# Attention kernel: which PSUM bank stands aside, and one feature turn a step sooner

## The chip, the cores and the metric

The kernel runs on one core of a Trainium2 chip. The metric is the device time of one execution in microseconds (us): the median of several runs. TensorE does the matmuls and writes only to PSUM, which has eight banks of 128 partitions x 512 float32 here (`ps[:, b, :]`). VectorE (DVE), ScalarE (ACT) and GpSimd (POOL) do the elementwise work, SyncE (SP) issues the weight transfers.

## The reference, cut to what matters

Two blocks one after the other on 256 tokens of width 1024, in float32. The first block has a pooling mixer and a dilated window attention (three groups of 16 heads). The second has two layers with modulation rows from a condition, each a mixer and an MLP; the first layer works on 256 tokens and 256 context tokens.

```python
# second block, layer 0: two attentions whose outputs stand side by side
o_a = gqa_attend(qa_x, ka_all, va_all)              # "A": 8 heads, 2 key heads
a = p[:, :, 0] - lam * p[:, :, 1]                   # "B": 4 heads, pairs of softmaxes
o_b = rms_norm(einsum('bhqs,bshe->bqhe', a, v), subln_g) * (1 - lam0)
out_x = concatenate([o_a, o_b], -1) @ w_out
# layer 1: "C" (window and sink, 8 heads), "D" (neighbourhood with bias, 8 heads)
# every layer: x = x + g1 * rms_norm(mixer); x = x + g2 * rms_norm(mlp)
```

## The kernel before, in words

Every float32 product is made of three matmuls of rounded high and low halves (`mm3`, lines 573 to 575; by halves at 620 and 622). Weights come as one stream of 1 MB chunks (`raw`, three slots, issued on SP at L539). ScalarE makes the high half (L1151), VectorE the low half (L1167); modulation rows use the raw chunk in TensorE directly (`mod`, L703). A chunk's slot is loaded again once it was used.

TensorE's program is one sequence of jobs written out by hand. `job(...)` (L561) gives a job its PSUM bank: the next of a list (`state["banks"]`, counter `turn[0]`), and makes TensorE wait until the job that had the bank before was read. A bank's reader is ScalarE or VectorE, each with a fixed order of its own.

An attention (`attend`, L842) runs over items, each a head and a tile of 128 queries. Step i issues the scores of the items ahead (L755, for the first attention L747), then side jobs placed by step, then the turned probabilities (`turns`, L789) of item i - lag and the product with the values (`values`, L817) of item i - lag - 1. The lag is 3 in A and 2 elsewhere. A and the first attention issue the scores of two items in every other step; in B one item has two score tiles. In the kernel before the banks in an attention are:

- first attention: the list is 0 to 5; side jobs take 6 and 7 in turn (`side=1`) until step 24, when both go back into the list's head;
- A and B of layer 0: the list is the other seven in order of last use; bank 7 stands aside (`side=2`) for projection blocks spread over the steps: in A two query tiles of the next part (`query_block`), in B from step 8 the first output tile (`product_block`). After A bank 7 becomes the list's first, after B its last;
- C and D of layer 1: as the first attention, until step 16.

The jobs ahead of A, in order (from L1044): key tile 2, four turned features `n1` (L658), key tile 3, query tile 0, query tile 1, in the midst of which the turned queries 2 and 3 and keys 2 and 3 (`turn_heads`, L1022) stand. Then A's step 0 issues the scores of items 0 and 1 and key tile 0, step 1 key tile 1. A query tile is read by ScalarE (L1595, squares) and then by VectorE (`head_sums`: L2334 and two of L2339); a turned tile is read by ScalarE (L1583).

In B, `side_steps_pairs` (L452) places turns of the feature-wise mixer output `fo` for the output projection: turn 0 in step 5, turn 1 in step 6, turns 2 and 3 in steps 16 and 17. A turn is four transposes (L658), a copy of the high half on ScalarE (L1215) and the low half on VectorE (L1777), which is the bank's last read. In a step VectorE does the maxima of two score tiles (L1998), combines the pair of the item before (L2043, L2044, L2046; this gives the probabilities), reads the output of item i - 4 (L2064) and makes the low half of a turn of that step. ScalarE copies the turned probabilities (L1340), makes the exponents (L1321) and then the turn's high half.

Of the kernel before, what the change touches and what calls it, by code (L numbers as in the profile page):

```python
# [278 lines left out]
def build(nc, T, out, counts):  # L279
    did, after = counts.did, counts.after  # L280
    with ExitStack() as ctx:
# [74 lines left out]
        mix = tile(ctx, "mix", [P, 4, D])  # L356
# [95 lines left out]
        def side_steps_pairs():  # L452


            return ([(1, ("v2", 0, 1, 0)), (3, ("v2", 0, 1, 1))] + [(at, ("fo", j)) for j, at in enumerate((5, 6, 16, 17))]
                    + [(8 + k, ("product", k)) for k in range(4)]
                    + [(18 + n, ("weights", PLACE[UNIT["out2", 0, 1].w0] + n)) for n in range(2)])

# [95 lines left out]
        def _(pe):  # L554
            mm = nc.tensor.matmul
            last = {}
            turn = [0, 0, 0]
            state = {"banks": list(range(8))}

            def job(*label, side=0):  # L560

                banks = (state["banks"], (6, 7), (7,))[side]
                b = banks[turn[side] % len(banks)]
                turn[side] += 1
                if b in last:
                    pe.wait_ge(*after("read", *last[b]))
                last[b] = label
                counts.banks[label] = b
                return ps[:, b, :]
# [75 lines left out]
                    ins = mm(o[:, 0:rhs.shape[-1]], lhs, rhs, start=True, stop=True)  # L645
                ins.then_inc(*did("tensor", ("read", "spin", label)))

            def turn_feature(name, src, tiles, ready, j):

                o = job(name, j)  # L650
                if j == 0:
                    for r in ready:
                        pe.wait_ge(*after(*r))
                for q in range(2):
                    for i, t in enumerate(tiles):
                        k = 2 * j + q
                        c = (2 * q + i) * P
                        ins = nc.tensor.transpose(o[:, c:c + P], src(t)[:, k * P:k * P + P], ident[:, :])  # L658
                ins.then_inc(*did("tensor", (name, j)))
# [6 lines left out]
            def turn_mixed(l, g, j):  # L666

                tiles = (2 * g, 2 * g + 1)
                ready = []
                if j == 0:  # L670
                    ready = [("mixed out" if l else "first half out", l, t) for t in tiles]
                elif l == 0 and j == 2:
                    ready = [("mixed out", l, t) for t in tiles]
                for r in ready:
                    pe.wait_ge(*after(*r))
                turn_feature(("fo", l, g), lambda t: mix[:, t, :], tiles, [], j)

            pending = []

# [140 lines left out]
            def query_block(t, k):  # L820

                u, name = UNIT["q2", 0, 1], ("q2", 0, 1, t)
                o = job(*name, side=2) if k == 0 else ps[:, counts.banks[name], :]
                if t == 2:
                    wait_weights(u, k)
                ins = mm3(o, fhi[:, k, t * P:t * P + P], flo[:, k, t * P:t * P + P],
# [5 lines left out]
            def product_block(k):  # L832

                u, name = UNIT["out2", 0, 0], ("out2", 0, 0, 2)
                o = job(*name, side=2) if k == 0 else ps[:, counts.banks[name], :]
                wait_weights(u, k)
                wait_feature(("fo", 0, 1), k)
                mm3(o, fhi[:, k, 2 * P:3 * P], flo[:, k, 2 * P:3 * P],
                    whalf(whi, u, k, 0, NW), whalf(wlo, u, k, 0, NW), k == 0, False)

            def attend(items, mods, steps=()):

                lag = turned_behind(items)
                for i in range(len(items) + lag + 1):
# [1 line left out]
                    if i < len(items) and i % ahead == 0:  # L846
                        scores(items[i:i + ahead])
                    alone = items[0][0] in ("first", "C") and i >= len(items) - (8 if items[0][0] == "first" else 16)
                    if alone and len(state["banks"]) == 6:

                        state["banks"] = [6, 7] + [state["banks"][(turn[0] + n) % 6] for n in range(6)]
                        turn[0] = 0
                    for at, step in steps:
                        if step[0] in ("chunk", "bias", "weights", "roots", "ahead", "queries"):
                            continue
# [91 lines left out]
            for n in range(2):  # L947
                by_token(UNIT["gb", n], ("gb", n), range(XT))

            state["banks"] = list(range(6))  # L950
            attend(items_first(), [], side_steps())
            turn_mod()
            turn_features("fo1", lambda t: gb[:, t, :], (0, 1), [("gated", items_first()[-1])])
# [59 lines left out]
            for l in range(2):  # L1013
# [12 lines left out]
                for part in range(2 - l):  # L1026
# [32 lines left out]
                    beside = l == 1  # L1059
                    if beside:  # L1060
                        gate_rows(1)
                    if beside:
                        state["banks"] = list(range(6))
                    else:
                        oldest = [state["banks"][(turn[0] + n) % 8] for n in range(8)]
                        state["banks"], turn[0] = [b for b in oldest if b != 7], 0
                    attend(items_second(l, part), mods_second(l, part),
                           side_steps_last() if beside else side_steps_pairs() if part else side_steps_halves())
                    if l == 0:
                        oldest = [state["banks"][(turn[0] + n) % 7] for n in range(7)]  # L1070
                        state["banks"], turn[0] = oldest + [7] if part else [7] + oldest, 0
                    else:
                        state["banks"] = list(range(8))
                if l == 0:
                    for n in range(2):
                        by_token(UNIT["out2", 0, n], ("out2", 0, n), (2, 3), feat=None if n else ("fo", 0, 1), last=False,
# [42 lines left out]
                for t in range(XT):  # L1119
                    for n in range(2):  # L1120
                        held[t, n] = job("acc", t, n)
                state["banks"] = [b for b in range(8) if b not in [counts.banks[("acc", t, n)] for t in range(2) for n in range(2)]]
                mlp_out(1, 0, range(2), ns=(0,), last=False)
                turn_hidden(1, 1)
                mlp_out(1, 0, range(2), ns=(1,), first=False)
# [1614 lines left out]
```

## Time and profile before

| | |
|---|---|
| median of three runs | 1545.56 us (1544.12 to 1545.67) |
| the profiled execution | 1544.99 us, span 1543.0 us |
| TensorE busy | 1508.7 us, 98% |
| TensorE weight loads busy | 1251.7 us, 81% |
| VectorE, ScalarE, GpSimd busy | 59%, 43%, 11% |
| granted clock of TensorE | 0.999 of full over the span |
| weight stream | 210 transfers of 1 MB, mean 151 GB/s |

The span is the time between the first and the last instruction; the device time has some 2 us more. A busy TensorE is not one at its peak, as its records are modelled and overlap. A row of the order of time gives start, duration, engine, line, tiles (out<-in), shape and count, and in brackets the idle time before it with the engine and line that ended it.

### The profile page before, as it was taken

Reading aid. Unit: us, or ns where it says so; the run is one execution under the profiler, and the core shown is the slowest. Engines: PE = TensorE matmul, PEld = TensorE weight load, DVE = VectorE, ACT = ScalarE, POOL = GpSimd, SP = SyncE. Lnnn points to the kernel's source line nnn. Section 1 sums busy time; section 2 is a strip of 40 time slices with the busy share of each in tenths; the row PEclk is TensorE's granted clock in tenths of the full one; section 3 lists DMA queues with packets and bytes.
Section 4 is the critical chain, followed back from the end, with each engine's and each line's share of the span. In section 5 each row is a group of like instructions: output and inputs, shape, how many; then the busy total and the mean of one; then the engine's idle time right before and its main releaser. Section 6 shows DMA issues by size and latency. Waiting matters only on the chain.

```text
span 1543.0 us, 22914 instructions
## 1 busy us (share of the span) xinstructions
PE 1508.7 (98%) x8906; PEld 1251.7 (81%) x8906; DVE 904.6 (59%) x1550; ACT 656.3 (43%) x1025; POOL 166.9 (11%) x179
## 2 busy tenths in 40 slices
PE   9999999999999998999999999999999999999998
PEld 7998698889897775786899777777787887778886
DVE  5785674756565883546675343333448646667655
ACT  5464334444444544536554222231224546654342
POOL 2200220000000120001223100111012020001010
PEclk9999999999999999999999999999999999999999
DMA  6456564453536225220232353443512421155451
GB/s 246 187 203 235 223 224 174 172 191 141 188 124 259 110 95 209 110 79 32 83 137 96 128 213 144 183 181 147 201 72 92 148 76 55 69 177 219 182 199 55
DMA packets 43765, 233.73 MB, mean 151 GB/s; under 512 B 13265, under 2 KB 14225, under 8 KB 16785
## 3 DMA queue, kind: packets, MB, share of 16 engines
q1 hardware_dynamic: 31232, 222.38, 38.4%
q10 hardware_dynamic: 12432, 9.94, 2.2%
q8 instruction: 72, 1.18, 0.3%
q14 instruction: 29, 0.23, 0.0%
HBM read 231.22 MB, written 1.08 MB: 151 GB/s over the span
## 4 chain that ended last, share of the span: by engine, by line
PE 86%; DVE 8%; ACT 2%; issue 1%; POOL 1%; DMA 1%; SPq 0%; DVEq 0%; ACTq 0%
PE ps L573 19%; PE ps L575 19%; PE ps L574 19%; PE ps L620 9%; PE ps L817 5%; PE ps L622 4%; PE ps L789 3%; DVE wlo L1167 3%; PE ps L755 2%; PE ps L703 2%; PE ps L747 2%; POOL f L2580 1%; DMA raw<-in_wstream 1%; PE ps L687 1%; ACT whi L1151 1%
## 5 line engine op out<-in xcount | busy, mean ns | idle before, releaser
L1167 DVE TENSOR_TENSOR wlo<-raw,whi 128x2048 fp32r<-128x2048 f32 x150 | 347.0, 2333 | 186.8 <-ACT whi L1151 186.5
L1151 ACT ACTIVATE whi<-raw 128x2048 fp32r<-128x2048 f32 x162 | 305.4, 1907 | 236.8 <-PE ps L575 162.4
L573 PE MATMUL ps<-whi,f 128*128 128x512 f32 (+1 forms) x624 | 221.9, 356 | 6.4 <-DVE dev L1815 2.6
L575 PE MATMUL ps<-whi,f 128*128 128x512 f32 (+1 forms) x624 | 216.1, 346 | 0.0
L574 PE MATMUL ps<-wlo,f 128*128 128x512 f32 (+1 forms) x624 | 215.8, 346 | 0.0
L573 PE MATMUL ps<-f,whi 128*128 128x256 f32 (+1 forms) x640 | 206.8, 323 | 1.8 <-DVE wlo L1167 1.6
L620 PE MATMUL ps<-f,whi 128*128 128x512 f32 x576 | 203.1, 400 | 2.8 <-DVE kq L1983 1.6
L575 PE MATMUL ps<-f,wlo 128*128 128x256 f32 (+1 forms) x640 | 205.0, 320 | 0.0
L574 PE MATMUL ps<-f,whi 128*128 128x256 f32 (+1 forms) x640 | 204.9, 320 | 0.0
L573 PE MATMUL ps<-whi,hhi 128*128 128x512 f32 x384 | 152.6, 397 | 0.0
L575 PE MATMUL ps<-whi,hlo 128*128 128x512 f32 x384 | 151.9, 395 | 0.0
L574 PE MATMUL ps<-wlo,hhi 128*128 128x512 f32 x384 | 151.8, 395 | 0.0
L573 PEld LDWEIGHTS ps<-whi,f 128*128 128x128 f32 x624 | 118.1, 189 | 33.3 <-issue 9.6
L622 PE MATMUL ps<-f,wlo 128*128 128x256 f32 x504 | 141.4, 280 | 0.0
L573 PEld LDWEIGHTS ps<-f,whi 128*128 128x128 f32 x640 | 121.8, 190 | 20.3 <-issue 6.5
L575 PEld LDWEIGHTS ps<-whi,f 128*128 128x128 f32 x624 | 118.1, 189 | 14.9
L575 PEld LDWEIGHTS ps<-f,wlo 128*128 128x128 f32 x640 | 121.9, 190 | 8.9
L574 PEld LDWEIGHTS ps<-f,whi 128*128 128x128 f32 x640 | 121.9, 190 | 8.6
L574 PEld LDWEIGHTS ps<-wlo,f 128*128 128x128 f32 x624 | 118.3, 190 | 12.6
L620 PEld LDWEIGHTS ps<-f,whi 128*128 128x128 f32 x576 | 104.8, 188 | 27.7 <-issue 3.8
L2591 POOL TENSOR_TENSOR hlo<-htmp,hhi 128x256 fp32r<-128x256 f32 (+1 forms) x64 | 60.5, 945 | 423.9 <-ACT hhi L1518 423.9
L622 PEld LDWEIGHTS ps<-f,wlo 128*128 128x128 f32 x504 | 95.2, 189 | 2.5
(282 smaller groups left out, 2147.5 us busy)
## 6 DMA issues: line engine op xcount, KB each, us to landing
raw<-in_wstream SPq DMA_DIRECT2D x210, 1024.0 KB, 4.9
gates<-gated ACTq DMA_DIRECT2D x6, 512.0 KB, 4.2
hx<-in_x SPq DMA_DIRECT2D x1, 1024.0 KB, 5.4
lnrow<-in_ln_g ACTq DMA_DIRECT2D x2, 512.0 KB, 4.1
lnrow<-in_ln_b ACTq DMA_DIRECT2D x2, 512.0 KB, 5.7
hc<-in_ctx ACTq DMA_DIRECT2D x1, 1024.0 KB, 5.5
mix<-in_rpb_rows ACTq DMA_DIRECT2D x4, 256.0 KB, 4.4
hc<-in_rpb_rows ACTq DMA_DIRECT2D x4, 256.0 KB, 3.8
```

Of the source, the lines that this page charges most:

```text
L573: mm(o, lh, rh, start=start, stop=False)
L574: mm(o, lh, rl, start=False, stop=False)
L575: return mm(o, ll, rh, start=False, stop=stop)
L620: ins = mm(both, wh, parts_f[:, :, k, c0:c0 + S], start=k == 0, stop=k == KD - 1)
L622: mm(o[:, 0:S], wl, fhi[:, k, c0:c0 + S], start=False, stop=False)
L703: ins = mm(o[at:at + 32, :], condz[:, 2 * k:2 * k + 32], raw[:, c % RAW_SLOTS, base:base + NW], start=k < 4, stop=k >= 4, tile_position=(0 ...
L747: ins = mm(o, kq1[po:po + DH, l % 2, 1, j * 2 + tq, t * P:t * P + P], kq1[po:po + DH, l % 2, 0, j * 2 + tq, 0:n], start=True, stop=True)
L789: ins = nc.tensor.transpose(o[:, (j - b) * P:(j - b + 1) * P], e[:, j * P:j * P + P], ident[:, :])
L817: ins = mm(o[:, 0:dv], p[:, i % 2, j * P:j * P + P], v, start=j == 0, stop=j == kt - 1)
L1151: nc.scalar.activation(whi[:, w % SPLIT_SLOTS, :], raw[:, c % RAW_SLOTS, :], ACT.Copy, scale=QSCALE if SPLIT[w][0].name[0] == "q" else 1.0 ...
L1167: ins = nc.vector.tensor_tensor(low, raw[:, c % RAW_SLOTS, :], high, ALU.subtract)
L2591: p.tensor_tensor(hlo[:, j % 2, e, cols], htmp[:, e % 2, cols], hhi[:, j % 2, e, cols].bitcast(F32), ALU.subtract).then_inc(*did("pool", * ...
```

## The change

It rewrites how banks are put aside. `set_aside(n)` takes the n banks used longest ago out of the list, for side jobs; `bring_back` puts them at the list's head, or at its end. Lists are turned so that their first is the one used longest ago, also after the last accumulators have taken their banks. A side job with nothing aside takes from the list with the list's counter. In A and B the bank aside is thus no longer always bank 7. The turns 0 and 1 of `fo` in B take the bank aside, and turn 0 goes from step 5 to step 4, on TensorE, ScalarE and VectorE.

```diff
-            return ([(1, ("v2", 0, 1, 0)), (3, ("v2", 0, 1, 1))] + [(at, ("fo", j)) for j, at in enumerate((5, 6, 16, 17))]
+            return ([(1, ("v2", 0, 1, 0)), (3, ("v2", 0, 1, 1))] + [(at, ("fo", j)) for j, at in enumerate((4, 6, 16, 17))]
...
-            turn = [0, 0, 0]
-            state = {"banks": list(range(8))}
+            turn = [0, 0]
+            state = {"banks": list(range(8)), "aside": []}
+
+            def oldest_first():
+                return [state["banks"][(turn[0] + n) % len(state["banks"])] for n in range(len(state["banks"]))]
+
+            def set_aside(n):
+                banks = oldest_first()
+                state["aside"], state["banks"], turn[:] = banks[:n], banks[n:], [0, 0]
+
+            def bring_back(last=False):
+                banks = oldest_first()
+                state["banks"] = banks + state["aside"] if last else state["aside"] + banks
+                state["aside"], turn[:] = [], [0, 0]
 
             def job(*label, side=0):
-                banks = (state["banks"], (6, 7), (7,))[side]
+                side = 1 if side and state["aside"] else 0
+                banks = state["aside"] if side else state["banks"]
                 b = banks[turn[side] % len(banks)]
...
-                turn_feature(("fo", l, g), lambda t: mix[:, t, :], tiles, [], j)
+                turn_feature(("fo", l, g), lambda t: mix[:, t, :], tiles, [], j, side=1 if (l, g) == (0, 1) and j < 2 else 0)
...
-                o = job(*name, side=2) if k == 0 else ps[:, counts.banks[name], :]
+                o = job(*name, side=1) if k == 0 else ps[:, counts.banks[name], :]
...
-                    if alone and len(state["banks"]) == 6:
-                        state["banks"] = [6, 7] + [state["banks"][(turn[0] + n) % 6] for n in range(6)]
-                        turn[0] = 0
+                    if alone and state["aside"]:
+                        bring_back()
...
-            state["banks"] = list(range(6))
+            set_aside(2)
             attend(items_first(), [], side_steps())
...
-                    if beside:
-                        state["banks"] = list(range(6))
-                    else:
-                        oldest = [state["banks"][(turn[0] + n) % 8] for n in range(8)]
-                        state["banks"], turn[0] = [b for b in oldest if b != 7], 0
+                    set_aside(2 if beside else 1)
                     attend(items_second(l, part), mods_second(l, part),
                            side_steps_last() if beside else side_steps_pairs() if part else side_steps_halves())
-                    if l == 0:
-                        oldest = [state["banks"][(turn[0] + n) % 7] for n in range(7)]
-                        state["banks"], turn[0] = oldest + [7] if part else [7] + oldest, 0
-                    else:
-                        state["banks"] = list(range(8))
+                    if not beside:
+                        bring_back(last=part == 1)
...
-                state["banks"] = [b for b in range(8) if b not in [counts.banks[("acc", t, n)] for t in range(2) for n in range(2)]]
+                standing = [counts.banks[("acc", t, n)] for t in range(2) for n in range(2)]
+                state["banks"], turn[0] = [b for b in oldest_first() if b not in standing], 0
```

## Rows read from the trace of the kernel before

**Rows 1.** The page: busy time by engine, TensorE's granted clock in 40 slices
```profile
PE 1508.7 (98%) x8906; PEld 1251.7 (81%) x8906; DVE 904.6 (59%) x1550; ACT 656.3 (43%) x1025; POOL 166.9 (11%) x179
...
PEclk9999999999999999999999999999999999999999
```

**Rows 2.** TensorE's waits over the whole span: total, times, longest, in us
```profile
PE ps L620 <- DVE kq L1983: 1.6, 1, 1.6
```

**Rows 3.** First attention in order of time, TensorE and then VectorE
```profile
471.50 1.92 PE L703 MATMUL ps<-raw,condz 128*32 128x512 f32 x16
473.71 0.52 PE L789 MATMUL ps<-ident,e 128*128 128x128 f32 x3 [0.30 <-DVE modsum L1906]
...
473.39 0.18 DVE L1906 TENSOR_REDUCE modsum<-ps 128x8 f32<-128x32 f32 x1
```

**Rows 4.** A attention's start, TensorE in order of time
```profile
561.73 0.70 PE L755 MATMUL ps<-kT,qT 64*128 64x256 f32 x4
562.73 0.38 PE L573 MATMUL ps<-whi,f 128*128 128x256 f32 x1 [0.30 <-DVE mix L2339]
...
565.71 0.28 PE L573 MATMUL ps<-whi,f 128*128 128x256 f32 x1
```

**Rows 5.** The same stretch on VectorE
```profile
561.93 0.74 DVE L2339 TENSOR_TENSOR mix<-ps,ropeg 128x256 f32<-128x256 f32 x2
...
564.64 0.74 DVE L2339 TENSOR_TENSOR mix<-ps,ropeg 128x256 f32<-128x256 f32 x2
...
567.60 0.29 DVE L2329 TENSOR_REDUCE hss<-e 128x2 f32<-128x128 f32 x1 [0.63 <-ACT e L1595]
...
569.41 0.76 DVE L1998 TENSOR_REDUCE nmax<-ps 128x1 f32<-128x256 f32 x2 [0.61 <-PE ps L755]
...
571.19 2.28 DVE L1167 TENSOR_TENSOR wlo<-raw,whi 128x2048 fp32r<-128x2048 f32 x1
```

**Rows 6.** The chain near 574 us (start, us, what), and TensorE at 582
```profile
574.50 7.63 DMA raw<-in_wstream
...
582.17 1.06 PE L703 MATMUL ps<-raw,condz 128*32 128x512 f32 x8 [1.24 <-DMA raw<-in_wstream]
```

**Rows 7.** B attention, TensorE in order of time
```profile
707.62 0.70 PE L755 MATMUL ps<-kT,qT 64*128 64x256 f32 x4
...
710.38 0.63 PE L658 MATMUL ps<-ident,mix 128*128 128x128 f32 x4 [0.40 <-DVE mix L2064]
...
712.15 0.70 PE L755 MATMUL ps<-kT,qT 64*128 64x256 f32 x4 [0.48 <-ACT e L1321]
...
713.82 0.71 PE L817 MATMUL ps<-vv,p 128*128 128x128 f32 x4 [0.17 <-DVE f L1777]
715.69 0.70 PE L755 MATMUL ps<-kT,qT 64*128 64x256 f32 x4 [1.15 <-DVE mix L2064]
...
719.00 0.38 PE L789 MATMUL ps<-ident,e 128*128 128x128 f32 x2
```

**Rows 8.** B attention, VectorE in order of time
```profile
709.89 0.35 DVE L2064 TENSOR_SCALAR mix<-ps,rinv 128x128 f32<-128x128 f32 x1
710.15 0.75 DVE L1998 TENSOR_REDUCE nmax<-ps 128x1 f32<-128x256 f32 x2
...
711.66 0.35 DVE L2064 TENSOR_SCALAR mix<-ps,rinv 128x128 f32<-128x128 f32 x1
713.08 0.69 DVE L1777 TENSOR_TENSOR f<-ps,f 128x512 fp32r<-128x512 f32 x1 [1.07 <-ACT f L1215]
...
716.01 0.69 DVE L1777 TENSOR_TENSOR f<-ps,f 128x512 fp32r<-128x512 f32 x1 [0.47 <-ACT f L1215]
...
718.12 0.35 DVE L2064 TENSOR_SCALAR mix<-ps,rinv 128x128 f32<-128x128 f32 x1
...
729.67 1.29 DVE L1998 TENSOR_REDUCE nmax<-ps 128x1 f32<-128x512 f32 x2 [0.63 <-PE ps L755]
```

**Rows 9.** B attention, ScalarE in order of time: the turn's copy
```profile
712.44 0.60 ACT L1215 ACTIVATE f<-ps 128x512 fp32r<-128x512 f32 x1
```

More of the change, by code:

```diff
@@ L646, in spin, with turn_feature @@
                 ins.then_inc(*did("tensor", ("read", "spin", label)))
-            def turn_feature(name, src, tiles, ready, j):
-                o = job(name, j)
+            def turn_feature(name, src, tiles, ready, j, side=0):
+                o = job(name, j, side=side)
                 if j == 0:
@@ L834, in product_block @@
                 u, name = UNIT["out2", 0, 0], ("out2", 0, 0, 2)
-                o = job(*name, side=2) if k == 0 else ps[:, counts.banks[name], :]
+                o = job(*name, side=1) if k == 0 else ps[:, counts.banks[name], :]
                 wait_weights(u, k)
```

## The prediction

> **What bounds the kernel now.** The page's first part comes first [rows 1]: TensorE is busy for 1508.7 of 1543.0 us, and its granted clock is at the full level (2.4 GHz) in every slice. All its idle time is 34.3 us, so no edit of banks can be worth more; what matters is which single waits of TensorE it removes or makes. The view of TensorE's waits says who ended them: its largest by a key tile of the first attention is 1.6 us [rows 2]; in the A attention it is exponents of ScalarE and one weight transfer, in the pairwise (B) attention VectorE's reads of outputs. Then I read the order of time at three places, TensorE's side and the releaser's [rows 3 to 9].
>
> A job starts when the job that had its bank before was read. So two times count for each: when TensorE could come to it, and when the bank's last read ended. The change computes the same; it pairs jobs with other banks and brings one turn forward. I went through the jobs in the code's order, gave each its bank by the old and by the new rule, and looked where the new last read ends after TensorE comes, and where an old wait of that kind goes. Three places came out.
>
> **First attention.** Two banks stand aside before and after, and each side job follows the side job two before it, as now: the 1.6 us wait stays. What changes is behind the banks' return at step 24. Before, a turn of the modulation row still counted over banks 6 and 7 by itself although both were back in the list, and the second job after it was given the bank it had just filled: the transposes at 473.71 idle 0.30 us for the read that starts at 473.39 and takes 0.18 [rows 3]. After, the turn is counted with the others and the transposes get an output's bank that was read long before. They follow the 16 modulation matmuls (471.50, 1.92 us) directly. Bounds 0 and 0.3; I take 0.3, as TensorE has no other wait for the next 20 us.
>
> **A attention, the new wait.** The last eight takers of banks before it are, oldest first: the fourth turned feature of n1, key tile 3, query tile 0, query tile 1, two query turns, two key turns. Before, the list without bank 7 gives the first score the feature's bank, the second key tile 3's, and key tile 0 of step 0 query tile 0's. The trace bears it out: that tile's first matmul (562.73) idles 0.30 us for L2339 [rows 4], which is query tile 0's last read, two instructions from 561.93 in 0.74 us, over at 562.67 [rows 5]. After, the oldest bank is the one set aside and all move up one: the scores get key tile 3's and query tile 0's banks, key tile 0 gets query tile 1's. Its last read is the same pair of instructions at 564.64, over at 565.38 [rows 5], and VectorE, which has no idle time ahead of it, can't do it sooner. So the scores wait from 561.73 to 562.7, and the key tile starts at 565.42 (0.04 behind the read, as 562.73 is to 562.69) instead of 562.73: 2.7 us. Both waits lie on one path, so it is 2.7 and not 2.7 + 1.0.
>
> Queued behind it on TensorE are key tile 1 (565.71, its new bank a query turn's, long read) and all of step 2. Who waits for these: VectorE idles 0.63 us at 567.60 for ScalarE's square of key tile 0 and 0.61 us at 569.41 for step 2's scores, and from there runs through to the low half of weights at 571.19 [rows 5], which releases a weight slot. The transfers behind it are issued by 574.50 and land 7.63 us later, and TensorE idles 1.24 us for them at 582.17 [rows 6]. So the transfers are issued 2.7 us later too, and the idle time stays 1.24: that is why I count nothing of the 2.7 as absorbed. What idle time follows in A is for exponents of scores that TensorE itself issued, and shifts with it. Bounds: 2.7, and 2.7 - 1.24 = 1.5 if the transfer came at its old time. I take 2.7.
>
> **B attention, the moved turn.** Now turn 0 of `fo` stands in step 5 and takes the next of seven banks, whose output is read by 710.24 (709.89 + 0.35): it starts at 710.38 after 0.40 us idle. Its bank then holds up a product by 0.17 us, and the scores of steps 6 and 7 idle 0.48 and 1.15 us for the banks of outputs 1 and 2 [rows 7]. In all 2.20 us of TensorE's idle time lie here. After, in the old frame of time (all is 2.4 us later by then):
> - The turn stands behind step 4's scores (707.62 and some 0.64) and its bank was read long ago: 708.26 to 708.70 (its issue takes 0.46 here: 710.38 to the next 710.84). Step 5's scores start at 709.48.
> - ScalarE's exponents of step 4 come 0.25 later, as the turned probabilities ahead of them do. Its copy follows and ends at 711.0 [rows 9]. VectorE reads output 0 by 710.24 as now, waits for the copy, and makes the low half from 711.04 to 711.73. Step 5's maxima then start at 711.64 instead of 710.15, and output 1 is read by 713.50 instead of 712.01 (711.66 + 0.35) [rows 8].
> - Step 6's scores no longer need that bank: 711.14 instead of 712.15. Turn 1 follows when turn 0's low half is done, 711.9. But step 6's turned probabilities need output 1's bank: 713.6, 0.3 later than now. The wait has moved by one job.
> - Step 7's scores start at 714.40 instead of 715.69, its turns when output 2 is read (715.28), at 715.42.
> - Step 8's turns need output 3. VectorE waits 0.80 and 0.65 us for the two copies where it waited 1.07 and 0.47, so it is only 0.1 earlier here: output 3 is read by 718.40 (718.12 + 0.35 - 0.08), start 718.50 instead of 719.00 [rows 7, 8].
>
> So of the 2.20 us only 0.5 come through: VectorE's order, not the banks, is what ends last. From 719.00 on TensorE has no idle time up to step 12's scores and keeps the 0.5; VectorE idles 0.63 for those scores at 729.67 [rows 8], which then come 0.5 sooner, and carries it on. Bounds: 0.1 (VectorE's share alone) and 2.2 (every wait gone); I take 0.5. The turn's own time, ScalarE's 0.60 and VectorE's 0.69 are the same work moved by a step; none of it issues anything on SP's or POOL's queue.
>
> **The rest.** C/D takes the two oldest banks instead of 6 and 7, and the list behind the last accumulators is in another order. Every job there that comes within 0.5 us of its bank's last read has the same predecessor before and after: 0.
>
> **Sum.** -0.3 + 2.7 - 0.5 = +1.9 us. Against the profiled execution's 1544.99 (its span 1543.0 and 1.99 around it) this is 1546.9; that execution lies 0.57 under the median of three, 1545.56, so for a median the forecast is 1547.4. That is +0.12%, less than the 0.2% (3.1 us) that a measurement of this kernel can tell from no change.
>
> **The rivals.**
> - *The wait in A is absorbed.* For it: an idle time of 1.24 us for a transfer stands close behind. Against: the transfer's issue hangs on VectorE, which waits for the late tiles. It gives 1547.4 - 1.24 = 1546.2. Chance 0.12.
> - *No new wait in A, or all of B's go.* If the list stood otherwise at A's start: 1547.4 - 2.7 = 1544.7; with all of B's 2.2 besides: 1543.0. Against: the 0.30 us row names the query tile. Chance 0.08.
> - *Slower, by the order on VectorE in B.* Turn 0's low half now stands before step 5's maxima. If ScalarE's copy comes late, every later output read is late by it. It decides from the point where step 8's turns come after 719.00: the two waits for copies then add up to 2.0 us or more instead of 1.45. With one whole copy and low half (0.60 + 0.69) not hidden, B costs 0.8 instead of giving 0.5: 1548.7, and 1549.0 without the first attention's 0.3. Chance 0.13.
> - *The clock falls.* TensorE would idle 1.0 and 2.0 us around four short matmuls. After the trace's 1.6 us idle at a key tile the clock stayed at its full level [rows 1, 2]. Were it at 1.2 GHz for as much work as lies between 565.71 and A's first turns, some 5.4 us, that would cost up to 5.4: 1552.8. Chance 0.02. The Trainium skill ("TensorE: Matmul & The Clock Gate", section "A second HAM failure mode: psum-queue depth-cycling") says that cycling through PSUM banks can leave TensorE idle so often that the clock swings between its levels. By that rule this rival, and against it the trace: B now has four such idle times within 6 us at the full clock.
> - *It doesn't do what it says*: the banks come out in another order than worked out, and the waits are as before, 1545.6. Chance 0.03.
>
> **How the numbers follow.** The forecast has 0.62, with a range of its own of 1546.3 to 1548.5. Faster by over 0.2% (under 1542.5) is a part of the second rival: 0.03. Slower by over 0.2% (over 1548.65): the third and fourth and 0.04 of the forecast's own spread, 0.19. Within it: 0.78. The range reaches down into the second rival and up through the third: 1543.9 to 1549.6.
>
> **What would show it.** In the profile after: around 561.4 to 565.1 the scores idle about 1 us and key tile 0 about 2, both for L2339; no wait of L789 for L1906; up to 690 everything later than before by 2.4. In B: turn 0 directly behind step 4's scores; in place of the 1.15 us of the scores (L755) for L2064 a wait of about 1.3 us of the probabilities' turns (L789) for L2064 in step 6; VectorE's two waits for L1215 together some 1.45 us. I would be wrong if the key tile waits under 1 us, or if the distance to before shrinks or grows between 570 and 600 us.

## The result, and the profile after

| | before | after |
|---|---|---|
| median of 10 runs each | 1545.80 us (1543.98 to 1547.30) | 1550.02 us (1548.61 to 1550.54) |
| ratio, 95% interval | | 1.0027 (1.0020 to 1.0035) |
| profiled execution, its span | 1544.99, 1543.0 us | 1549.87, 1548.0 us |
| granted clock over the span | 0.999 | 0.996 |

The changed kernel is slower, by 4.2 us in the medians and 4.9 us in the profiled executions. The forecast was 1547.4 us with a range up to 1549.6: the sign was right, the size was not, and the time lies 0.4 us outside the range.

The page of after, its line of busy times, has the same work on each engine as [rows 1] and 3.5 us more of TensorE's busy time. The same number of matmuls is busy for longer, so some of them ran slower:

```profile
PE 1512.2 (98%) x8906; PEld 1254.8 (81%) x8906; DVE 904.7 (58%) x1550; ACT 656.4 (42%) x1025; POOL 166.9 (11%) x179
```

Both kernels have 8906 records of matmuls in the same roles, so I subtracted the start of each one before from its start after. Below, "late" is that difference. These are the places at which it could move.

**First attention.** The matmuls of the modulation row stand at 471.33 now, and the transposes behind them no longer wait as in [rows 3]: late goes from -0.17 to -0.53. At 486.67 it is back at 0.00, where both kernels start the second half of the next modulation row. Now it idles there, for a transfer (TensorE in order of time):

```profile
486.67 1.07 PE L719 MATMUL ps<-raw,condz 128*32 128x512 f32 x8 [0.32 <-DMA raw<-in_wstream]
```

**A's start.** TensorE in order of time, the rows that answer [rows 4], and then the releaser on VectorE, which answers [rows 5]:

```profile
562.87 0.70 PE L771 MATMUL ps<-kT,qT 64*128 64x256 f32 x4 [1.03 <-DVE mix L2347]
565.49 0.58 PE L589 MATMUL ps<-whi,f 128*128 128x256 f32 x1 [1.91 <-DVE mix L2347]
...
566.29 0.41 PE L589 MATMUL ps<-whi,f 128*128 128x256 f32 x1
566.51 0.41 PE L590 MATMUL ps<-wlo,f 128*128 128x256 f32 x1
...
569.28 0.28 PE L591 MATMUL ps<-whi,f 128*128 128x256 f32 x1
569.40 0.28 PE L589 MATMUL ps<-whi,f 128*128 128x256 f32 x1
```
```profile
564.69 0.74 DVE L2347 TENSOR_TENSOR mix<-ps,ropeg 128x256 f32<-128x256 f32 x2
```

The scores (L771) wait 1.03 us and key tile 0 (L589) waits 1.91, both for a query tile's last read (L2347 is before's L2339, and starts at 564.69 as it did at 564.64). The key tile starts 2.75 us late. Then look at the distance of its matmuls, two rows with the same 256 columns: 0.22 us at 566.3, 0.12 us at 569.3. The view by stretches gives the granted clock (the fourth figure, behind the count: 1.00 is the full 2.4 GHz, 0.50 is 1.2 GHz):

```profile
core 0: us, PE busy (x), PEclk, DMA share, GB/s
561.00:565.00 4.00, 1.54 (x8) 1.00 0.68 252
565.00:569.00 4.00, 3.51 (x18) 0.57 0.03 10
569.00:573.00 4.00, 4.00 (x34) 1.00 0.00 0
```

From 565.1 to 568.5 the clock was at 1.2 GHz, behind two idle times with four short matmuls between them. At 568.43 late is 4.04: the fall, the stretch at the lower clock, cost 1.3 us more.

**The transfer at 582.17** [rows 6] is met at 586.10 with 1.11 us idle instead of 1.24, and late goes from 4.06 to 3.92.

**B.** TensorE in order of time, the rows that answer [rows 7]:

```profile
712.17 0.66 PE L674 MATMUL ps<-ident,mix 128*128 128x128 f32 x4
...
714.30 0.41 PE L805 MATMUL ps<-ident,e 128*128 128x128 f32 x2 [0.17 <-DVE mix L2072]
...
717.51 0.41 PE L805 MATMUL ps<-ident,e 128*128 128x128 f32 x2 [1.13 <-DVE mix L2072]
...
719.28 0.41 PE L805 MATMUL ps<-ident,e 128*128 128x128 f32 x2 [0.28 <-DVE mix L2072]
...
722.38 0.41 PE L805 MATMUL ps<-ident,e 128*128 128x128 f32 x2 [0.29 <-DVE mix L2072]
```

Turn 0 stands directly behind step 4's scores. The four waits of before, 2.20 us, are gone, and four others have come, 1.87 us, all of the transposes of p for VectorE's output reads (L2072, before's L2064). Late falls from 3.9 at 707.62 to 3.38 at 719.00. VectorE's waits for the two copies are 0.75 and 0.64 us, together 1.39 (1.45 forecast):

```profile
714.90 0.69 DVE L1785 TENSOR_TENSOR f<-ps,f 128x512 fp32r<-128x512 f32 x1 [0.75 <-ACT f L1223]
...
719.77 0.69 DVE L1785 TENSOR_TENSOR f<-ps,f 128x512 fp32r<-128x512 f32 x1 [0.64 <-ACT f L1223]
```

**Around 1360 us** both kernels idle some 2.4 us (2.34 before, 2.37 after) ahead of a first unit of the last MLP. Behind it the clock fell in after's profile (0.60 of full between 1364 and 1368 us) and not in before's; late goes from 3.5 to 5.0 and stays there.

The sum of the profiled executions: 0 + 2.75 + 1.3 - 0.1 (the transfer) - 0.5 + 1.6 = 5.05 us, beside 5.0 us between the spans. The last 1.6 looked as if it had nothing to do with the change; the experiments had to say that, and whether the 1.3 had.

### The profile page after: what moved, and what is told of

Read it like the earlier page. It is cut to its first block, busy times and chain, and to the rows that moved or that the text cites. A ratio compares the mean times of both kernels' runs of the same rounds, so it can differ in the third digit from the quotient of the medians.

```text
span 1548.0 us, 22914 instructions
## 1 busy us (share of the span) xinstructions
PE 1512.2 (98%) x8906; PEld 1254.8 (81%) x8906; DVE 904.7 (58%) x1550; ACT 656.4 (42%) x1025; POOL 166.9 (11%) x179
## 4 chain that ended last, share of the span: by engine, by line
PE 86%; DVE 8%; ACT 2%; DMA 2%; issue 1%; POOL 1%; SPq 0%; DVEq 0%; ACTq 0%
PE ps L589 19%; PE ps L591 19%; PE ps L590 19%; PE ps L636 9%; PE ps L833 5%; PE ps L638 4%; PE ps L805 3%; DVE wlo L1175 3%; PE ps L719 3%; PE ps L771 2%; DMA raw<-in_wstream 2%; PE ps L763 1%; POOL f L2588 1%; PE ps L703 1%; ACT whi L1159 1%
## 5 line engine op out<-in xcount | busy, mean ns | idle before, releaser
L589 PE MATMUL ps<-whi,f 128*128 128x512 f32 (+1 forms) x624 | 223.1, 357 | 8.1 <-DVE dev L1823 2.6
L589 PE MATMUL ps<-f,whi 128*128 128x256 f32 (+1 forms) x640 | 206.8, 323 | 1.8 <-DVE wlo L1175 1.6
L589 PE MATMUL ps<-whi,hhi 128*128 128x512 f32 x384 | 152.6, 397 | 0.0
L589 PEld LDWEIGHTS ps<-whi,f 128*128 128x128 f32 x624 | 119.1, 191 | 35.1 <-issue 9.0
L589 PEld LDWEIGHTS ps<-f,whi 128*128 128x128 f32 x640 | 121.8, 190 | 20.3 <-issue 6.5
```

Of the source, the lines that this page charges most:

```text
L589: mm(o, lh, rh, start=start, stop=False)
```

## The experiments

Each ratio is to runs of the kernel before on the same chip. Those runs have medians of 1545.57 us (experiments 1, 2, 4 and 5), 1545.71 (3, 6, 7 and 9), 1545.22 (8, 10 and 11) and 1545.84 (12), the last two on one chip. So where experiments from different sets are compared, some 0.6 us of a difference may be the set's. A ratio is not that of the two medians, and differs from it by up to 0.9 us.

**1. A's bank alone (a_fifth).** The changed kernel, in which A sets aside the bank that it had before.

```diff
-            def set_aside(n):
+            def set_aside(n, at=0):
                 banks = oldest_first()
+                banks = [banks[at]] + banks[:at] + banks[at + 1:] if at else banks
...
-                    set_aside(2 if beside else 1)
+                    set_aside(2 if beside else 1, at=0 if beside or part else 4)
```

> The changed kernel, but ahead of the A attention the fifth oldest bank is set aside (a query turn's, as before the change) instead of the oldest. Theory (the new wait for the query tiles' last reads and the lower clock behind it are the whole loss): the waits for L2339 shrink from 2.9 to 0.3 us, the clock does not fall near 565 us, and the time is about 2.7 + 1.3 = 4.0 us under the changed kernel's 1550.0, so 1545.4 to 1546.2, ratio to before 0.9998 to 1.0003. Rival (the loss has another place, such as the order of banks elsewhere): at least 1547.5, ratio over 1.001.

Measured: 1545.31 us (1542.95 to 1546.35), ratio 0.9994 (0.9985 to 1.0003). The key tile waits as in [rows 4], and no clock falls there (TensorE in order of time):

```profile
562.70 0.39 PE L590 MATMUL ps<-whi,f 128*128 128x256 f32 x1 [0.30 <-DVE mix L2348]
```

So one bank at one place holds the whole loss: in the medians 4.2 us above before with it, 0.3 below without. The rest of the change gives too little to be told from nothing.

**2. The other way round (before_a_oldest).** The kernel before, with only A's bank taken as the oldest.

```diff
-                banks = (state["banks"], (6, 7), (7,))[side]
+                banks = (state["banks"], (6, 7), state["one"])[side]
...
-                        state["banks"], turn[0] = [b for b in oldest if b != 7], 0
+                        state["one"] = (7,) if part else (oldest[0],)
+                        state["banks"], turn[0] = [b for b in oldest if b != state["one"][0]], 0
```

> The kernel before with one part of the change alone: in the A attention the bank set aside is the one used longest ago instead of bank 7. Theory: this makes the whole loss and nothing of the gains, so slightly slower than the changed kernel: 1545.8 + 2.7 + 1.3 = 1549.8, or 1550.2 if the changed kernel's B gain of 0.4 us is real; a clock fall behind the wait near 565 us. Rival (the loss comes from several parts): under 1548.5.

Measured: 1556.44 us (1554.31 to 1557.51), ratio 1.0071 (1.0057 to 1.0085). That is over 6 us more than either expectation, and more than the whole change costs. A's two waits and the fall of the clock behind them are there. But there is a new one, ahead of the first scores of layer 1's attention, which in before and after wait 0.62 us for a turned key tile. TensorE and then VectorE in order of time:

```profile
1214.30 1.22 PE L755 MATMUL ps<-kT_b,qT_b 64*128 64x512 f32 x2 [4.87 <-DVE grow L2159]
```
```profile
1208.87 2.29 DVE L1168 TENSOR_TENSOR wlo<-raw,whi 128x2048 fp32r<-128x2048 f32 x1
1211.56 2.29 DVE L1168 TENSOR_TENSOR wlo<-raw,whi 128x2048 fp32r<-128x2048 f32 x1 [0.40 <-ACT whi L1152]
1213.77 0.27 DVE L2159 COPY grow<-ps 32x128 f32<-32x128 f32 x1
```

By the releaser that the trace names, the scores got the bank of the gate row (`grow`) that TensorE had just filled, and VectorE reads that one behind two low halves of weights. The kernel before rotates over banks 0 to 5 there, a fixed list; which of them was used last depends on everything before, and A's other order shifted it. The clock fell behind this wait too, for another 1.5 us.

**3. The fixed banks at layer 1 alone (c_fixed).** To see whether that is it: the changed kernel with banks 6 and 7 aside at layer 1, as before had it.

```diff
-                    set_aside(2 if beside else 1)
+                    if beside:
+                        state["banks"], state["aside"] = list(range(6)), [6, 7]
+                    else:
+                        set_aside(1)
```

> The changed kernel, in which the attention of layer 1 (C, D) sets aside banks 6 and 7 as in the kernel before, and rotates over banks 0 to 5, instead of the two used longest ago. Theory (once A's rotation differs, the fixed banks at layer 1 no longer suit, and C's first scores wait for VectorE's gate rows, as in before_a_oldest): a wait of 4 to 5 us ahead of C's first scores at about 1210 us, 1553 to 1555 us. Rival (the loss in before_a_oldest came from the particular order that it left behind, which this kernel doesn't have): no new wait there, 1549.6 to 1550.4 us.

Measured: 1553.68 us (1553.31 to 1556.04), ratio 1.0057 (1.0041 to 1.0072). The same VectorE copy is waited for, one job later (TensorE in order of time):

```profile
1212.74 0.58 PE L589 MATMUL ps<-f,whi 128*128 128x256 f32 x1 [2.92 <-DVE grow L2171]
```

So the time is as expected and the wait, expected at 4 to 5 us, is 2.9; with the lower clock that its profile has behind it, the cost is 3.7 us in the medians (8.0 us above before, where after is 4.2). The part of the change that I had put at nothing is worth that much here: with A's order as the change makes it, a fixed list at layer 1 costs that again.

**4. The moved turn alone (turns_old).** The changed kernel with turns 0 and 1 back in steps 5 and 6 and in the rotation.

```diff
-[(at, ("fo", j)) for j, at in enumerate((4, 6, 16, 17))]
+[(at, ("fo", j)) for j, at in enumerate((5, 6, 16, 17))]
...
-                turn_feature(..., tiles, [], j, side=1 if (l, g) == (0, 1) and j < 2 else 0)
+                turn_feature(..., tiles, [], j)
```

> The changed kernel with turns 0 and 1 of fo back in steps 5 and 6 and in banks of the list. Theory (VectorE's order lets 0.5 us of the 2.2 through): 0.5 us slower than the changed kernel, 1550.5; the B attention's four idle times of the kernel before stand again. Rival (all idle time removed there would come through): 2.2 slower, 1552.2. Rival (the moved turn gives nothing): 1550.0.

Measured: 1549.61 us (1547.48 to 1550.82), ratio 1.0023 (1.0014 to 1.0032). The expected 1550.5 did not come: in the medians it isn't above after, so they don't show B's gain. The traces do: B's waits are before's again (0.41, 0.48, 0.17, 1.15 us), and against after's start of B it loses 0.5 us by the end of step 8. A half microsecond lies below what these runs resolve. (The granted clocks of its eleven runs average 0.9968, those of after's ten 0.9961. By my estimate after loses 1.1 us of full clock more by that, 0.0007 of 1548, which is enough to hide it.)

**5. The waits in A filled (wait_filled).** The changed kernel with 8 more matmuls of 256 columns ahead of A's first scores and 15 ahead of key tile 0, into the bank that stands aside. Nothing reads them.

```diff
+                    if i == 0 and items[0][0] == "A":
+                        fill(8, True, False)
...
+                            if at == i == 0:
+                                fill(15, False, True)
```

> The changed kernel with 8 matmuls of 256 columns ahead of A's first scores and 15 ahead of key tile 0, into the bank that stands aside, whose results nobody reads: some 2.7 us of TensorE work in the 2.9 us in which it would wait anyway. The waits and their ends stay where they are. Theory (the clock falls because TensorE idles): no clock fall near 565 us, key tile 0's matmuls 0.12 us apart again, and 1.3 us faster than the changed kernel, 1548.7. Rival (the fall has nothing to do with the idle time, or does not matter): the same as the changed kernel, 1550.0, or slower if the dummy work is in the way.

Measured: 1548.45 us (1547.00 to 1549.29), ratio 1.0015 (1.0006 to 1.0024), 1.6 us less than after (1.3 when the medians are taken against before's, 1.9 by the two ratios). The key tile starts no earlier, but now runs at the full clock. TensorE in order of time, and the stretch that had 0.57:

```profile
563.83 2.06 PE L862 MATMUL ps<-whi,f 128*128 128x256 f32 x15
565.82 0.39 PE L589 MATMUL ps<-whi,f 128*128 128x256 f32 x1
```
```profile
565.00:569.00 4.00, 4.00 (x34) 1.00 0.08 33
```

One profile could be luck, but the granted clocks of its eleven runs average 0.9980, like those of 89 runs of before (0.9979) and unlike those of after's ten (0.9961).

Experiment 3 gives the same split without added work, as c_fixed is the changed kernel up to layer 1. It has both waits and its clock stayed up (TensorE in order of time, and its stretch):

```profile
565.54 0.39 PE L589 MATMUL ps<-whi,f 128*128 128x256 f32 x1 [1.91 <-DVE mix L2352]
```
```profile
565.00:569.00 4.00, 3.46 (x29) 1.00 0.02 8
```

Between 555 and 579 us c_fixed loses 2.7 us to before, wait_filled 2.7 and after 4.0. So about 2.7 us are the wait for the bank, and 1.3 to 1.6 are the clock behind it.

**6. The kernel before, profiled again (before_again).**

> The kernel before, profiled again. If the half-clock stretch at about 180 or 1360 us belongs to idle times that both kernels have, it may show here too, though the first profile had none; near 565 us there is none, since TensorE isn't idle for longer than 0.3 us there. 1544 to 1547 us.

Measured: 1546.86 us, span 1544.9. Of the first two profiles only after's had a stretch at 1.2 GHz near 180 and near 1360 us. In this one the kernel before has both. The idle times ahead of them stand in before's first profile too, where the clock stayed up (TensorE in order of time):

```profile
178.48 1.94 PE L658 MATMUL ps<-ident,hx 128*128 128x128 f32 x16 [2.08 <-DVE hx L1954]
...
1359.34 0.47 PE L573 MATMUL ps<-whi,f 128*128 128x512 f32 x1 [2.34 <-DVE dev L1815]
```

The second profile's view by stretches (busy time of TensorE, its weight loads, VectorE, ScalarE and GpSimd, then granted clock, DMA share, GB/s):

```profile
178.00:183.00 5.00, 4.32 (x24) 3.63 (x28) 3.59 (x8) 1.26 (x2) 1.85 (x2) 0.66 0.93 392
1360.00:1364.00 4.00, 4.00 (x12) 3.14 (x11) 3.86 (x5) 1.09 (x2) 0.00 (x0) 0.57 0.90 314
```

The fall near 180 us costs 1.6 us and is given back by 187, where TensorE would else wait 0.91 and 0.28 us for GpSimd. The one at 1360 costs 1.6 against before's first profile and stays. So the last 1.6 us of the sum above belong to neither kernel: an execution of either has them or not.

**7. The long idle times filled (kept_busy).** a_fifth with matmuls of 128 columns in the two idle times that both kernels have.

```diff
                 o = job(name, j, side=side)
+                if name == "f1" and j == 0:
+                    for _ in range(14):
+                        mm(o[:, 0:P], ident[:, :], ident[:, :], start=True, stop=True)
```

and 16 of the same ahead of the unit at 1355 us.

> The changed kernel with A's bank as before (a_fifth), and matmuls of 128 columns, never read, put into the two longest idle times of TensorE outside A: 14 ahead of the first turn at about 178 us (idle 2.08 us), 16 ahead of the first unit at about 1355 us (idle 2.37 us). They go into the bank that the next group overwrites. Theory (the clock at 1.2 GHz follows an idle time, and at these two places falls in some executions only): the granted clock stays at 2.4 GHz at both, for up to 1.3 us where it fell before; the median falls 0.3 to 1.3 us below a_fifth's 1545.3, so 1544.0 to 1545.0 us. Rival (the fall is not tied to the idle time, or the matmuls themselves delay the path): 1545.3 to 1546.0 us, and a half-clock stretch at the same places.

Measured: 1545.19 us (1544.89 to 1545.75), ratio 1.0000 (0.9991 to 1.0009). The clock stayed at its full level in the profile, and the spread of eleven runs fell from a_fifth's 3.4 us to 0.9. The clock is as the theory had it; the median, expected at 1544.0 to 1545.0, didn't move. The filling was too long (3.39 us of matmuls in an idle time of 2.08 us), which experiment 8 tests.

**8. The right amount (busy_half).** The same with 8 and 9.

> kept_busy with 8 and 9 matmuls instead of 14 and 16: there each was recorded as two of 0.12 us, so that the 28 took 3.39 us of an idle time of 2.08 us and the 32 took 3.73 us of 2.37 us, and TensorE itself came 1.1 to 1.2 us late. Now they take 1.9 and 2.1 us. Theory: the granted clock stays at 2.4 GHz at both places, without the delay: about 1 us below kept_busy's 1545.2, so 1543.6 to 1544.4 us, with a spread of the runs under 1.5 us (that of a_fifth is 3.4 us). Rival (the delay cost nothing, or a clock that falls there costs nothing): 1545.0 to 1545.5 us.

Measured: 1544.36 us (1543.98 to 1544.91), ratio 0.9992 (0.9983 to 1.0001). TensorE in order of time, and its granted clock (1.00) by stretch:

```profile
1356.47 2.17 PE L612 MATMUL ps<-ident 128*128 128x128 f32 x18
1358.85 0.50 PE L590 MATMUL ps<-whi,f 128*128 128x512 f32 x1 [0.21 <-DVE wlo L1182]
```
```profile
1360.00:1364.00 4.00, 4.00 (x23) 1.00 0.83 297
```

It is 0.8 us below kept_busy, near the 1 us expected (0.3 when the medians are taken against before's on each chip, 1.2 by the two ratios); the spread stays at 0.9 us. But the fastest runs of a_fifth (1542.95) and of before (1543.24) are faster than its fastest: the filling takes away the slow executions, and also something from the fastest. The second row also corrects a reading of the profiles without filling, here a_fifth's (TensorE, then VectorE):

```profile
1358.03 0.47 PE L590 MATMUL ps<-whi,f 128*128 128x512 f32 x1 [2.37 <-DVE dev L1824]
```
```profile
1355.59 2.29 DVE L1176 TENSOR_TENSOR wlo<-raw,whi 128x2048 fp32r<-128x2048 f32 x1
```

They put this idle time down to `dev`, a short VectorE operation. In busy_half the releaser is the low half of the next weights, and in a_fifth that one too ends just ahead, at 1357.88.

**9. VectorE's order in B (low_later).** The claim of the prediction's working was that VectorE's order, not the banks, ends last in B. a_fifth, with the low halves of turns 0 and 1 made one step later:

```diff
-                        if at == i and step[0] == "fo":
+                        if step[0] == "fo" and at + (1 if step[1] < 2 else 0) == i:
                             low_feature(("fo", 0, 1), 1, step[1])
```

> The changed kernel with A's bank as the kernel before has it (a_fifth), and VectorE makes the low halves of feature turns 0 and 1 one step later than ScalarE makes the high ones. The operations are the same and only VectorE's order in B differs. Theory (what ends last in B is VectorE's order, not the bank): VectorE no longer stands 0.74 us and 0.64 us waiting for ScalarE's high half, and TensorE's wait for VectorE before the transposes of p behind turn 1 (1.13 us) falls under 0.5 us; 0.6 to 1.4 us less than a_fifth's 1545.3, so 1543.9 to 1544.7 us. Rival (the low half of 0.69 us is only paid a step later, where VectorE again ends last): 1545.0 to 1545.6 us, the idle time moved to a later step.

Measured: 1544.62 us (1542.77 to 1546.00), ratio 0.9993 (0.9984 to 1.0002). The wait of 1.13 us and those behind it are gone, and two of another kind have come (TensorE in order of time):

```profile
711.33 0.66 PE L675 MATMUL ps<-ident,mix 128*128 128x128 f32 x4 [0.90 <-DVE f L1786]
...
715.84 0.50 PE L590 MATMUL ps<-whi,f 128*128 128x512 f32 x1 [0.69 <-DVE f L1786]
```

B gets 0.35 us shorter than a_fifth's by this (-0.64 at its start, -0.98 behind step 8); the other 0.6 between the two profiles is the transfer at 581 us, which TensorE met without waiting. The claim holds for the waits of the transposes; the gain in the trace is smaller than expected, since turn 1 now waits for turn 0's low half in the one bank aside. The median lies within the expected 1543.9 to 1544.7, but in the profile the transfer gave more of it than B.

**10. Turn 1 back in the rotation (low_list).** low_later with only turn 0 aside (`j < 1`), to take those two waits away.

> low_later, with feature turn 1 in a bank of the rotation and only turn 0 in the bank aside. In low_later TensorE waits 0.90 us ahead of turn 1 and 0.69 us ahead of the first product block, both for the low half that frees the bank aside. Theory: both waits go (the bank aside is free, the next bank of the rotation was read some 2 us earlier) and VectorE is next: 0.7 to 1.5 us below low_later's 1544.6, so 1543.1 to 1543.9 us. Rival (VectorE is the bound of these steps, so the time comes back ahead of the transposes of p): 1544.3 to 1544.8 us.

Measured: 1546.92 us (1546.22 to 1548.75), ratio 1.0013 (1.0004 to 1.0022), 2.3 us above low_later (2.8 when the medians are taken against before's). TensorE in order of time:

```profile
711.47 0.66 PE L675 MATMUL ps<-ident,mix 128*128 128x128 f32 x4 [0.30 <-DVE mix L2073]
...
713.93 0.70 PE L772 MATMUL ps<-kT,qT 64*128 64x256 f32 x4 [1.14 <-DVE mix L2073]
...
717.39 1.53 PE L772 MATMUL ps<-kT,qT 64*128 64x512 f32 x4 [1.94 <-ACT subtmp L1399]
```

Both expectations fall. The two waits are gone, but a turn in the rotation of seven moves every later job to a bank that was used one job later, and scores wait 1.14 and 1.94 us. The releaser named for the second reads no bank; turn 1's low half ends 0.25 us before it (716.46, 0.68), and which bank it was I didn't settle. Behind it the clock fell again (718.0), and 1546.9 follows.

**11. Both (low_list_busy)** is low_list with busy_half's matmuls.

> low_list with the matmuls of busy_half. Theory: the two gains lie at different places and add: 1541.8 to 1543.2 us, below both kernels. Rival (one of them is taken back by a transfer behind it, as the first attention's 0.3 us was): 1543.5 to 1544.5 us.

Measured: 1548.17 us (1547.05 to 1549.84), ratio 1.0017 (1.0008 to 1.0026), outside both expectations. Its base had already lost; at 718.4 us the clock stayed low for twice as long as in low_list. Filling the idle times elsewhere doesn't help against a fall that has its own idle time.

**12. The best of the parts (low_later_busy)** is low_later with 8 and 8 matmuls.

> low_later (A's bank as before, the low halves of turns 0 and 1 a step later) with 8 and 8 of the matmuls of busy_half. Theory (the two lie at different places and add): busy_half's 1544.4 less low_later's 0.7 us, so 1543.3 to 1544.0 us, with a spread under 1.5 us and a clock of 1.0, faster than the kernel before by 0.1%. Rival (the time saved in B shifts the later work against the transfers and the clock, as in low_list_busy, which came out 1.3 us above low_list): 1544.4 to 1546 us.

Measured: 1544.22 us (1543.90 to 1544.94), ratio 0.9989 (0.9980 to 0.9998). It falls between the two expectations. It is the fastest median, and the only one below before's whose interval excludes no change; the gain is 0.1%. The granted clock is 0.999 or 1.0 in all eleven runs, which fits a gain from the clock but does not size it. VectorE's order adds 0.1 us to busy_half's 1544.36, less than can be told from nothing.

## Why the prediction was wrong

- *First attention, -0.3.* The wait went as said (0.36 us), but it did not reach the end. The step that failed is "TensorE has no other wait for the next 20 us": it looked only at waits that before had, and with TensorE earlier the weight transfer became the later one, 13 us on. The profiles of after, a_fifth, wait_filled and low_list_busy have 0.32, 0.39, 0.42 and 0.58 us idle there. In all eleven profiles of kernels with this part of the change the 0.36 are there at 474 us, and 0.2 to 0.8 us are lost again by 555. So the net lies between 0.2 us gained and 0.5 lost, never at the 0.3 forecast.
- *A's new wait, +2.7.* Right: 1.03 and 1.91 us idle, 2.75 us late, by the releaser named. Experiment 1 took the wait away and the loss went with it.
- *The transfer absorbs nothing.* Right for after (1.11 us against 1.24). But this idle time isn't fixed by the kernel's order: before has 1.24 and 1.33 in its two profiles, a_fifth and low_later, which are alike up to there, have 0.46 and under 0.1, and after, c_fixed and turns_old, again alike, have 1.11, 1.22 and 0.86.
- *B, -0.5.* Right in size and in its parts: the 1.13 us wait of the transposes, the copies' 1.39, 0.5 us in all. It can be read in the traces only; the medians of experiment 4 don't resolve it.
- *The rest, 0.* In after no new wait came at layer 1, as said. What the sentence missed is that this part of the change does something: without it, experiment 3, the change costs 3.7 us more.
- *The clock.* This is the main step that failed: the sum has no term for it, and the runs show 1.3 to 1.6 us. It stood among the rivals with a chance of 0.02 and a price of up to 5.4 us, and the argument against it was a single idle time of 1.6 us and B's four shorter ones, behind which one profile had the clock up. That profile also has idle times of 2.08 and 2.34 us with the clock up; the second profile of before has the clock down behind both. So one profile without a fall says little. The case was another, too: two idle times close together with almost no work between. In three of the four profiles with that pair the clock fell (after, turns_old and before_a_oldest; not c_fixed), for 1.3 to 1.5 us; experiment 5 filled the idle time without shortening the wait and had 1.3 to 1.9 us back. The chance was far too low, the price four times too high. The Trainium skill ("TensorE: Matmul & The Clock Gate", section "A second HAM failure mode: psum-queue depth-cycling") describes idle times from cycling through PSUM banks that make the clock swing between its levels. The trace of after agrees in part: behind 1.03 and 1.91 us of waiting for banks the clock fell once, and did not swing.
- *The base.* before's single profile (1544.99) had neither of the two falls of the clock that before_again had (1546.86). A span with the clock up at both places is not the median execution, and the step from it to the median (0.57 us) hid that. (The sum gives 1547.46, which the prediction writes as 1547.4.)

With the clock's 1.3 and without the first attention's 0.3 the sum would have been 3.5 us, 1549.1, or 1549.3 on the 1545.80 that before measured beside after. The last 0.7 us to 1550.0 isn't shown by any run. Two causes are at hand. The two weight transfers, at 487 and 582 us, move a profile by up to 1.2 us. And the granted clocks (0.9961 on average against before's 0.9979, each rounded to 0.001) say that after loses 2.8 us of full clock more, where the stretch from 565.1 to 568.5 takes 1.7. By this estimate an execution of after has more than one fall more than one of before.

## What to carry to other kernels

Which bank is "used longest ago" says when it was last given out, not when its last read ends: ask who reads it and where that read stands in its engine's queue, and shift the whole rotation in your head, since one more or one less taker moves every job behind it. A fixed list of banks that works may owe that to everything ahead of it. And when a change makes new idle time on TensorE, price it twice: the wait itself, and the matmuls behind it at half the clock.

## What the runs showed of the hardware

- TensorE's granted clock fell to 1.2 GHz behind idle times of 1.03 and 1.91 us with four matmuls between them (three of four profiles), of 1.14 and 1.94 us (low_list), of 2.08 us, of 2.3 to 2.4 us, of 2.92 us (c_fixed) and of 4.87 us (before_a_oldest). Behind 2.08 and 2.34 us it fell in one of two profiles of the same kernel. It did not fall at the places that were filled with unread matmuls (wait_filled for the pair; kept_busy, busy_half, low_later_busy and low_list_busy for 2.08 and 2.4 us).
- A fall cost 1.3 to 1.6 us where matmuls followed densely, and 0 to 0.3 us in the end where TensorE waited for another engine soon after (near 180 us).
- With the two idle times filled, 33 runs of three kernels spread by 0.9 to 1.0 us each; unfilled, the same kernel spread by 3.4 us and the kernel before by 3.9 (1543.24 to 1547.09 in one set). So most of what looked like noise goes away with these idle times. That it is the clock alone isn't shown: six runs of a_fifth with the same granted clock, 0.998, lie between 1542.95 and 1546.18. And low_list_busy, filled in the same way but with its own fall at 718 us, spreads by 2.8.
- A matmul of 128 float32 columns with the identity on both sides left two records of 0.12 us each: 14 of them took 3.39 us.
